# Selected attention's queries by token: x stationary, 16 of 64 columns rotated, turned by block

## The chip, the cores and the metric

The kernel runs on one core of a Trainium2 chip. Its metric is the device time in microseconds of one execution; the median of three runs stands for the kernel. The profile comes from one further execution. Its times start at the first instruction of the span.

## The reference, cut to what matters

One sequence of 512 tokens with 1024 features runs through two blocks. The first block's mixing part is where the change lies:

```python
h = rmsnorm(x, norm_mix_g)
proj = h @ w_in            # q 8x64, k 64, v 64, qi 4x64, ki 64, wi 4, glu 1024
q = partial_rope(q.reshape(bsz, seq, 8, 64), cos, sin)   # first 16 of 64 columns a head
# the same for k, qi, ki
# index scores: relu(qi . ki) weighted by wi; each query keeps its 128 best keys
logits = einsum('bqhd,bqkd->bqhk', q, k_sel) * 64 ** -0.5   # selected keys, causal
a_out = softmax(logits) @ v_sel
u = causal_dwconv(ga * sigmoid(gg), conv_b_w, conv_b_b)     # 31 taps, 512 channels
b_out = silu(layernorm(u))
x = x + concat([a_out, b_out]) @ w_out
```

`partial_rope` takes columns x1 = 0..7 and x2 = 8..15 of a head to x1 cos - x2 sin and x2 cos + x1 sin, and leaves the other 48 alone. After this come a cross-attention to 256 memory tokens (their keys and values, kc and vc, are made in fills during the selected attention), a feed-forward part, and the whole second block (a recurrent part, an attention without softmax, a feed-forward part). The diff touches none of these.

## The kernel before

Features lie on the partitions, tokens on the free axis, so an activation is a set of tiles of 128 x 512. Every projection is done in three passes on TensorE (PE) with a high and a low part of each operand: w_high x_high, w_high x_low, w_low x_high. Weights come in chunks of 128 x 1024 through two buffers (`weights_raw`, and by it `weights_high` and `weights_low`): SP issues the load, ACT makes the high part (`high`, L703), POOL subtracts (`low`, L625), PE multiplies (`chunk`, L1736). The cast of a chunk waits for the chunk two before it to be done.

Each engine walks the same list, `FIRST_PLAN` (L390 and on), and does what is its own in each item, strictly in that order. Items: ("tile", n, ...) is the n-th 128 columns of w_in (16 tiles: ki/wi, qi, k/v, glu and gate, and last q in 12 to 15); ("best",) is one round of the selection on DVE, three MAX8 and three replacements (L1291, L1294), 16 in all; ("chosen",) turns the scores into 0 or -1e30 (L1299); ("fill", n, ...) is half a chunk of the memory's keys or values (24 matmuls of 256 columns a chunk of kc); ("tap", i) is one tap of the convolution on DVE (L1235), 84 in all; ("product", i) is one on ACT (L788) that POOL adds (L674), 40 in all; steps 0 to 34 are the selected attention, 32 pairs of a block of 128 queries and a head: ("logits", j) on PE (L1953) and the mask on DVE (L1321) and exponential on ACT (L840), ("prob", j) the transposes by PE (L1961) and ACT's copy (L848), ("value", j) on PE (L1972).

The queries are made like every other tile: the weights stand in PE, x moves, ACT copies the tile of 128 columns x 512 tokens to `qT` (L763). The rotation of tile 12 + i is a matmul with a constant matrix `rotate` (("query_turn", 2 + i), L1920, 128x512 in full precision, two passes) into a bank of its own, and then on DVE three operations over 128x512 (`rope`, L1189 to L1191): bank x sine, qT x cosine, sum, though 48 of 64 columns are not changed by it. The sine and cosine tables lie by feature and hold 1/rms of each token. The index queries (tiles 1 and 2) are rotated in the same way, the keys similarly (`key_rope`).

Of the kernel before, what the change touches and what calls it, by code (L numbers as in the profile page):

```python
# [12 lines left out]
P = 128  # L13
T = 512
# [27 lines left out]
for _name, _n in GEMMS:  # L42
    CHUNK[_name], TILE[_name] = _c, _t
    _c += _n
    _t += _n // 2 if _name.startswith("down") or _name == "vc" else 2 * _n if _name in ("out", "oc", "out2") else _n
# [43 lines left out]
def build(nc, w8, w11, xT, memT, mem, positions, params, blockdiag, out):  # L89
    ctx = ExitStack()  # L90
    with ctx:
# [69 lines left out]
        wi = sb("wi", [P, QB, IDX_HEADS], where=s1)  # L161
        cosine = sb("cosine", [P, T], where=s1)
# [72 lines left out]
        angle = aux[4][:]  # L235
        x_square = ([aux[5][:]] + [gate[:, k] for k in range(1, 4)] + [score[:, k] for k in range(3)]
# [45 lines left out]
        rotated = sem("rotated")  # L282
        roped = sem("roped")
# [102 lines left out]
        def adds_before(i):  # L386
# [4 lines left out]
                      ("tile", 3, 2, 5), ("spread",), ("key_turn", 0), ("query_turn", 0), ("tile", 3, 5, KB),  # L391
                      ("wi",), ("query_turn", 1), ("mem_scale", 0, 4), ("key", 0), ("query", 0), ("query", 1),
                      ("tile", 4, 0, KB), ("mem_scale", 4, 8)]
        for n in range(len(INDEX)):
# [9 lines left out]
                   11: [("glu_scale", 7), ("glu", 2), ("best",), ("product", 2)],  # L404
                   12: [("gate", 3), ("best",), ("product", 3), ("product", 4)],
                   13: [("glu", 3), ("best",), ("best",), ("query", 2), ("product", 5)],
                   14: [("best",), ("query", 3), ("product", 6), ("product", 7)],
                   15: [("best",), ("best",), ("query", 4), ("product", 8), ("product", 9)]}
        FIRST_PLAN += BETWEEN[5]
        for n in range(6, 16):  # L410
            FIRST_PLAN.append(("tile", n, 0, 4))
            if n >= 13:
                FIRST_PLAN.append(("query_turn", n - 11))
            FIRST_PLAN += [("tile", n, 4, KB)] + BETWEEN[n]
# [37 lines left out]
        BANKS = [item for item in FIRST_PLAN if item[0] in ("prob", "heads")]  # L452
# [127 lines left out]
        def _(pool):  # L580
# [14 lines left out]
            for t in (rotate, twice, rotate_twice, causal, strict, ident16):  # L595
# [5 lines left out]
                                 fill=-1.0, base=-8, pattern=[[-HALF, 2], [-1, 8]], channel_multiplier=1))  # L601
# [9 lines left out]
                                 fill=-1.0, base=-8, pattern=[[0, 2], [-1, 8]], channel_multiplier=1))  # L611
# [81 lines left out]
        def _(act):  # L693
# [54 lines left out]
            def tile_ends(n):  # L748

                if n < 4:  # L750
                    dst = (None, None, qiT[:, 1], kv[:])[n]
                elif n < 12:
                    b = n // 2 - 2
                    dst = gate[:, b] if n % 2 else glu[:, b, TAPS - 1:TAPS - 1 + T]
                else:
                    dst = qT[:, n - 12]
                tile_done(n // 2, n % 2)
                if n < 4:
                    a.copy(dst, acc[:, n % 2]).then_inc(tile_out[n % 2], 1)
                    high_next(n // 2, n % 2)  # L760
                else:
                    high_next(n // 2, n % 2)
                    a.copy(dst, acc[:, n % 2]).then_inc(tile_out[n % 2], 1)  # L763
# [27 lines left out]
            for what, *n in FIRST_PLAN:  # L791
# [343 lines left out]
        def _(dve):  # L1135
# [102 lines left out]
            for what, *n in FIRST_PLAN:  # L1238
# [4 lines left out]
                elif what == "spread":  # L1243
                    dve.wait_ge(x_spread, 1)
                    dve.wait_ge(tables_ready, 1)
# [20 lines left out]
                elif what == "query":  # L1266
                    t = qiT[:, j] if j < 2 else qT[:, j - 2]
                    dve.wait_ge(table_copied, 1)
                    rope(t, t, aux[4][:], aux[2 + j if j < 2 else j - 2][:])
# [444 lines left out]
        def _(pe):  # L1714
# [112 lines left out]
            def in_tile(n, k, end):  # L1827
                m, s = n // 2, n % 2
                if k == 0:
                    free(s, m)  # L1830
                chunk(m, s, end, s, A, first=k)

# [31 lines left out]
            def bank_free(*item):  # L1864

                at = BANKS.index(item)
                if at >= 2:
                    kind, j = BANKS[at - 2]
                    if kind == "heads":
                        pe.wait_ge(inverse_out, j + 1)  # L1870
                    else:
                        pe.wait_ge(probT_ready, j + 1)
# [18 lines left out]
            for what, *n in FIRST_PLAN:  # L1891
# [12 lines left out]
                elif what == "spread":  # L1904
                    pe.wait_ge(x_factor, 1)
                    spread(tok_factor, aux[5]).then_inc(x_spread, 1)
                elif what == "key_turn":
                    if j:
                        pe.wait_ge(rel_used, len(INDEX))
                    pe.wait_ge(tile_out[j], (1, 2)[j])  # L1910
# [4 lines left out]
                elif what == "query_turn":  # L1915
                    tile = 1 + j if j < 2 else 10 + j
                    pe.wait_ge(tile_out[tile % 2], tile // 2 + 1)
                    if j >= 2:
                        pe.wait_ge(roped, 4)
                    t_.matmul(aux[2 + j if j < 2 else j - 2][:], rotate[:], qiT[:, j] if j < 2 else qT[:, j - 2],  # L1920
                              start=True, stop=True).then_inc(rotated, 1)
# [24 lines left out]
                elif what == "logits":  # L1946
                    qb, h = DSA[j]
                    if j < A_HEADS:
                        pe.wait_ge(roped, 5 + h // 2 if j >= 2 else 6)
# [5 lines left out]
                elif what == "prob":  # L1955
                    pe.wait_ge(prob_raw, j + 1)
                    if j < 2:
                        pe.wait_ge(roped, 8)
# [379 lines left out]
```

## Time and profile before

| what | us |
|---|---|
| median of three runs | 1372.78 (1372.58 to 1373.69) |
| the profiled execution, its own time | 1372.61 |
| its span, first to last instruction | 1370.6 |
| PE busy | 1331.1 |
| DVE busy | 790.1 |
| POOL busy | 612.0 |
| ACT busy | 549.5 |

A busy time is the time in which an engine had an instruction under way. Matmuls overlap, so two of 0.39 us may start 0.23 us apart: starts are what to count. PE is near full for the whole span; the others are not, but they hold PE up where the work of a stage hangs on them. So the table only says that PE's idle time and PE's own instructions matter.

### The profile page before, as it was taken

The numbers are of one execution on the slowest core, as the hardware profiler recorded it, in microseconds if no ns is written. First come the engines' busy times: TensorE is split into PE (matmuls) and PEld (weight loads), VectorE is DVE, ScalarE is ACT, GpSimd is POOL, SyncE is SP. The second block draws the span as 40 slices with busy tenths as digits, with TensorE's granted clock in tenths as the row PEclk, the third lists the DMA queues.
The fourth block names the chain that finished last, engine by engine and source line by source line (L and its number), as shares of the span: only waits on it lengthen the run. The fifth ranks groups of instructions, "written<-read, shape, count | busy, mean of one in ns | idle before, by whom it ended". The sixth has DMA issues, their size and how long they took to land. (4 is left out here: it accounts for less than half of the span.)

```text
span 1370.6 us, 18053 instructions
## 1 busy us (share of the span) xinstructions
PE 1331.1 (97%) x6189; PEld 1079.0 (79%) x6189; DVE 790.1 (58%) x1097; ACT 549.5 (40%) x860; POOL 612.0 (45%) x299
## 2 busy tenths in 40 slices
PE   8998889999999999999999999899999999999997
PEld 6787766887678888888888777688788888888886
DVE  7788896632456777777533588677543333332222
ACT  5444776542343222323323254455442233232322
POOL 4597873332234444444444534132344444444441
PEclk9999999999999999999999999999999999999999
DMA  6122321221122222323322222111122222233222
GB/s 227 62 93 93 108 75 34 92 78 62 46 92 88 98 92 96 103 92 109 106 87 97 92 77 77 46 47 62 62 93 92 97 102 92 92 109 105 95 87 80
DMA packets 31875, 121.19 MB, mean 88 GB/s; under 512 B 3536, under 2 KB 3664, under 8 KB 31568
## 3 DMA queue, kind: packets, MB, share of 16 engines
q1 hardware_dynamic: 31536, 119.81, 25.9%
q8 instruction: 32, 0.52, 0.2%
q10 hardware_dynamic: 288, 0.69, 0.2%
q14 instruction: 19, 0.16, 0.0%
HBM read 118.40 MB, written 2.10 MB: 88 GB/s over the span
## 5 line engine op out<-in xcount | busy, mean ns | idle before, releaser
L625 POOL TENSOR_TENSOR weights_low<-weights_raw,weights_high 128x1024 fp32r<-128x1024 f32 (+1 forms) x204 | 526.4, 2581 | 725.3 <-ACT weights_high L703 725.1
L703 ACT CAST weights_high<-weights_raw 128x1024 fp32r<-128x1024 f32 (+1 forms) x202 | 221.9, 1099 | 504.7 <-PE acc L1736 475.1
L1736 PE MATMUL acc<-a_high,weights_high 128*128 128x512 f32 x976 | 390.5, 400 | 1.8 <-DVE a_low L1398 1.1
L1736 PE MATMUL acc<-a_high,weights_low 128*128 128x512 f32 x976 | 380.6, 390 | 0.0
L1736 PE MATMUL acc<-a_low,weights_high 128*128 128x512 f32 x976 | 380.3, 390 | 0.0
L1736 PEld LDWEIGHTS acc<-a_high,weights_high 128*128 128x128 f32 x976 | 183.7, 188 | 44.1 <-issue 3.7
L1736 PEld LDWEIGHTS acc<-a_low,weights_high 128*128 128x128 f32 x976 | 183.7, 188 | 39.3 <-issue 2.6
L1736 PEld LDWEIGHTS acc<-a_high,weights_low 128*128 128x128 f32 x976 | 183.5, 188 | 38.7
L1208 DVE TENSOR_TENSOR residual<-acc,residual 128x512 f32<-128x512 f32 (+1 forms) x63 | 43.3, 687 | 168.4 <-PE acc L1736 129.8
L1736 PE MATMUL acc<-h_high,weights_high 128*128 128x512 f32 x330 | 128.9, 391 | 0.0
L1736 PE MATMUL acc<-h_high,weights_low 128*128 128x512 f32 x330 | 128.4, 389 | 0.0
L1736 PE MATMUL acc<-h_low,weights_high 128*128 128x512 f32 x330 | 128.4, 389 | 0.0
L1480 DVE TENSOR_TENSOR h_low<-work,h_high 128x512 f32 x44 | 88.9, 2020 | 39.5 <-ACT h_high L953 39.5
L1474 DVE TENSOR_TENSOR work<-acc,row_factor 128x512 f32<-128x512 f32 x44 | 30.4, 691 | 105.5 <-PE acc L1736 105.5
L1736 PEld LDWEIGHTS acc<-h_high,weights_low 128*128 128x128 f32 x330 | 61.9, 188 | 13.0
L1736 PEld LDWEIGHTS acc<-h_high,weights_high 128*128 128x128 f32 x330 | 62.0, 188 | 12.7
L1736 PEld LDWEIGHTS acc<-h_low,weights_high 128*128 128x128 f32 x330 | 62.0, 188 | 12.5
L950 ACT ACTIVATE work<-work 128x512 f32<-128x512 f32 x44 | 27.8, 631 | 96.7 <-DVE work L1471 93.5
L1394 DVE TENSOR_TENSOR square_sum<-square_sum,square 128x512 f32<-128x512 f32 x19 | 54.9, 2891 | 18.0 <-ACT square L1104 9.1
L1235 DVE SCALAR_TENSOR_TENSOR aux<-glu,par,aux 128x512 f32<-128x512 f32 x78 | 58.7, 753 | 1.7
L1469 DVE SCALAR_TENSOR_TENSOR work<-gated,par,work 128x512 f32<-128x512 f32 x22 | 55.4, 2518 | 3.4 <-DVE work L1467 3.4
L674 POOL TENSOR_TENSOR conv<-conv,product 128x512 f32<-128x512 f32 x38 | 49.4, 1300 | 10.4 <-ACT product L788 9.0
(384 smaller groups left out, 1932.8 us busy)
## 6 DMA issues: line engine op xcount, KB each, us to landing
weights_raw<-w SPq DMA_DIRECT2D x172, 512.0 KB, 3.2
weights_raw<-w SPq DMA_DIRECT2D x32, 704.0 KB, 4.1
residual<-xT SPq DMA_DIRECT2D x8, 256.0 KB, 6.1
out<-y_tok SPq DMA_DIRECT2D x4, 512.0 KB, 3.1
mem_raw<-memT SPq DMA_DIRECT2D x1, 1024.0 KB, 5.3
mem_tok<-mem SPq DMA_DIRECT2D x1, 1024.0 KB, 7.5
lru_weights<-blockdiag ACTq DMA_DIRECT2D x1, 512.0 KB, 3.3
sine<-positions SPq DMA_DIRECT2D x1, 256.0 KB, 6.7
```

Of the source, the lines that this page charges most:

```text
L625: g.tensor_tensor(weights_low[:, s, 0:cols], weights_raw[:, s, 0:cols], weights_high[:, s, 0:cols].bitcast(F32), ALU.subtract).then_inc(we ...
L674: g.tensor_tensor(conv[:, b], conv[:, b], product[:, j % 2], ALU.add).then_inc(last_conv_steps, 1)
L703: a.copy(weights_high[:, s, 0:cols], weights_raw[:, s, 0:cols]).then_inc(weight_high, 1)
L950: a.activation(work[:, 0], work[:, 0], ACT.Silu).then_inc(silu_ready, 1)
L1208: v.tensor_tensor(residual[:, bass.ds(n, 1)].rearrange("p a n -> p (a n)"), acc[:, s], residual[:, bass.ds(n, 1)].rearrange("p a n -> p (a ...
L1235: ins = v.scalar_tensor_tensor(dst, src, weight, sofar, ALU.mult, ALU.add)
L1394: v.tensor_tensor(total_ if to is None else to, total_, squares, ALU.add).then_inc(summed, 1)
L1469: own.then(v.scalar_tensor_tensor(work[:, 0], gated[:, 1:1 + T], dcol("fconv_w", c + 1), work[:, 0], ALU.mult, ALU.add))
L1474: v.tensor_tensor(work[:, 1], acc[:, 1], row_factor[:], ALU.mult).then_inc(tile_out[1], 1)
L1480: v.tensor_tensor(at(dst_low, i), work[:, 1], at(dst_high, i).bitcast(F32), ALU.subtract).then_inc(operand_low, 1)
L1736: last = t_.matmul(acc[:, bank, 0:cols], w[:, s, wide], x_[:, k0 + k, 0:cols], start=start and k == opens and n == 0, stop=stop and k == c ...
```

## The change

- Chunks 12 to 15 of w_in are stored in another layout: rows of 128 features with all 512 query columns, two such rows a chunk. In `query_chunk` a block of 128 tokens of x is the stationary operand and 512 columns of weights move. The four blocks of tokens add up in four banks (`aux[0]` to `aux[3]`) over all 96 matmuls.
- ACT copies each block out with the token's factor 1/rms (`query_out`), into the space of the index queries and keys, now unused. By token, a head's 16 rotated columns are a strided view; DVE rotates only these (`query_rope`, three operations of 128 elements a partition). PE turns the block with four transposes and ACT copies it to `qT` (`query_back`).
- The tables by token come at the start: eight transposes of 16 x 128 and a copy on ACT (`tables`), ahead of the spread of the token factors. The sign of the sine moves from the matrix into the frequencies.
- Block 0 is turned ahead of the first logits, blocks 1 to 3 in steps 1 to 6. The logits of block qb wait for its copy into `qT`.
- The four rotation matmuls and twelve 128x512 operations of the queries go. The selection rounds stand one or two places earlier in the list.
- Eight of the 84 taps come ahead of step 0; the other 76 are spread over the same 31 steps.

```diff
         FIRST_PLAN = [("tile", 0, 0, KB), ("tile", 1, 0, KB), ("tile", 2, 0, KB), ("tile", 3, 0, 2), ("sum",),
-                      ("tile", 3, 2, 5), ("spread",), ("key_turn", 0), ("query_turn", 0), ("tile", 3, 5, KB),
+                      ("tile", 3, 2, 5), ("tables",), ("spread",), ("key_turn", 0), ("query_turn", 0), ("tile", 3, 5, KB),
...
-                   11: [("glu_scale", 7), ("glu", 2), ("best",), ("product", 2)],
-                   12: [("gate", 3), ("best",), ("product", 3), ("product", 4)],
-                   13: [("glu", 3), ("best",), ("best",), ("query", 2), ("product", 5)],
-                   14: [("best",), ("query", 3), ("product", 6), ("product", 7)],
-                   15: [("best",), ("best",), ("query", 4), ("product", 8), ("product", 9)]}
+                   11: [("glu_scale", 7), ("glu", 2), ("best",), ("best",), ("product", 2)],
+                   12: [("gate", 3), ("best",), ("best",), ("product", 3), ("product", 4)],
+                   13: [("glu", 3), ("best",), ("best",), ("product", 5)],
+                   14: [("best",), ("best",), ("product", 6), ("product", 7)],
+                   15: [("product", 8), ("product", 9)]}
...
-        FIRST_PLAN += FILLS[:1] + [("query_turn", 5), ("best",), ("query", 5), ("chosen",)]
-        FILLS = FILLS[1:]
-        FILLS_AT = (2, 1, 2, 1, 2, 1, 2, 1, 1, 1, 2, 1, 1, 1, 1, 1, 1, 1, 0, 1, 1, 0, 1, 0,
+        TAPS_AHEAD = 8
+        FIRST_PLAN += [("chosen",)] + [("tap", i) for i in range(TAPS_AHEAD // 2)]
+        FIRST_PLAN += [("query_out", b) for b in range(QB)] + [("query_rope", 0)] + FILLS[:2]
+        FIRST_PLAN += [("query_back", 0)] + [("tap", i) for i in range(TAPS_AHEAD // 2, TAPS_AHEAD)]
+        FILLS = FILLS[2:]
+        FILLS_AT = (1, 1, 2, 1, 2, 1, 2, 1, 1, 1, 2, 1, 1, 1, 1, 1, 1, 1, 0, 1, 1, 0, 1, 0,
...
             if step < CONV_STEPS:
-                FIRST_PLAN += [("tap", i) for i in range(step * len(CONV) // CONV_STEPS,
-                                                         (step + 1) * len(CONV) // CONV_STEPS)]
+                rest = len(CONV) - TAPS_AHEAD
+                FIRST_PLAN += [("tap", TAPS_AHEAD + i) for i in range(step * rest // CONV_STEPS,
+                                                                      (step + 1) * rest // CONV_STEPS)]
+            if step in (1, 3, 5):
+                FIRST_PLAN.append(("query_rope", (step + 1) // 2))
+            if step in (2, 4, 6):
+                FIRST_PLAN.append(("query_back", step // 2))
...
+                elif what == "tables":
+                    act.wait_ge(tables_turned, 1)
+                    a.copy(token_tables[:].rearrange("p a b r -> p (a b r)"), aux[0][:, 0:2 * QB * 16]
+                           ).then_inc(token_tables_out, 1)
+                elif what == "query_out":
+                    if j < QB - 1:
+                        act.wait_ge(q_done, j + 1)
+                    else:
+                        act.wait_ge(chunk_done, 16)
+                    act.wait_ge(x_factor, 1)
+                    a.activation(q_tok[j], aux[j][:], ACT.Copy, scale=tok_factor[:, j:j + 1]).then_inc(q_out, 1)
+                elif what == "query_back":
+                    act.wait_ge(q_turned, j + 1)
+                    a.copy(qT[:, :, j * P:(j + 1) * P], turn_bank(what, j)[:].rearrange("p (n t) -> p n t", t=P)
+                           ).then_inc(q_ready, 1)
...
+                elif what == "query_rope":
+                    dve.wait_ge(token_tables_out, 1)
+                    dve.wait_ge(q_out, j + 1)
...
+                    own.step(v.tensor_tensor(turned_, heads_[:, :, ::-1, :], sines, ALU.mult))
+                    own.then(v.tensor_tensor(straight, heads_, cosines, ALU.mult))
+                    v.tensor_tensor(heads_, turned_, straight, ALU.add).then_inc(q_roped, 1)
...
+            def query_chunk(n, i):
+
+                if n == 12 and i == 0:
+                    pe.wait_ge(roped, 4)
+                pe.wait_ge(weight_low, n + 1)
+                for b in range(QB):
+                    rows, wide = slice(b * P, (b + 1) * P), slice(i * T, (i + 1) * T)
+                    for p_, (w, x_) in enumerate(((weights_high, a_high), (weights_high, a_low),
+                                                  (weights_low, a_high))):
+                        last = t_.matmul(aux[b][:], x_[:, 2 * (n - 12) + i, rows], w[:, n % 2, wide],
+                                         start=n == 12 and i == 0 and p_ == 0,
+                                         stop=n == 15 and i == 1 and p_ == 2)
+                    if n == 15 and i and b < QB - 1:
+                        last.then_inc(q_done, 1)
+                if i:
+                    last.then_inc(chunk_done, 1)
...
+                elif what == "tables":
+                    pe.wait_ge(tables_ready, 1)
+                    for i, table in enumerate((sine, cosine)):
+                        for b in range(QB):
+                            at = (i * QB + b) * 16
+                            last = t_.transpose(aux[0][:, at:at + 16], table[0:16, b * P:(b + 1) * P],
+                                                ident[0:16, 0:16])
+                    last.then_inc(tables_turned, 1)
+                elif what == "query_back":
+                    pe.wait_ge(q_roped, j + 1)
+                    if j == 0:
+                        pe.wait_ge(q_out, QB)
+                    bank_free(what, j)
+                    blocks_of(q_tok[j], turn_bank(what, j)).then_inc(q_turned, 1)
...
-                    if j < A_HEADS:
-                        pe.wait_ge(roped, 5 + h // 2 if j >= 2 else 6)
+                    if h == 0:
+                        pe.wait_ge(q_ready, qb + 1)
...
-    starts += every[:4]
+    queries = w_in[:, 0:T].reshape(4, 2, P, T).transpose(0, 2, 1, 3).reshape(4, P, -1)
```

## Rows read from the trace of the kernel before

**Rows 1.** The page: busy time, share of the span, instructions.
```profile
PE 1331.1 (97%) x6189; PEld 1079.0 (79%) x6189; DVE 790.1 (58%) x1097; ACT 549.5 (40%) x860; POOL 612.0 (45%) x299
```

**Rows 2.** Stretches (us from start:end): length, busy per engine, granted clock, DMA.
```profile
core 0: us, PE busy (x) PEld busy (x) DVE busy (x) ACT busy (x) POOL busy (x), PEclk, DMA share, GB/s
98.00:117.80 19.80, 19.80 (x84) 15.28 (x83) 14.40 (x36) 8.21 (x12) 17.08 (x12) 1.00 0.31 103
...
125.80:129.20 3.40, 0.00 (x0) 0.01 (x1) 3.29 (x8) 3.40 (x6) 2.48 (x2) 1.00 0.00 0
...
130.00:133.40 3.40, 3.40 (x19) 3.40 (x18) 0.01 (x1) 0.76 (x3) 3.40 (x3) 0.52 0.48 154
...
160.00:221.00 61.00, 54.53 (x308) 42.04 (x307) 56.36 (x104) 44.55 (x96) 42.59 (x28) 1.00 0.18 62
...
228.00:1370.60 1142.60, 1120.31 (x5105) 909.61 (x5103) 603.94 (x700) 415.17 (x605) 454.10 (x177) 1.00 0.26 86
```

**Rows 3.** Timeline of PE around a rotation: start, length, engine, line, operation, count.
```profile
101.24 0.39 PE L1736 MATMUL acc<-a_high,weights_low 128*128 128x512 f32 x1
101.47 1.02 PE L1920 MATMUL aux<-qT,rotate 128*128 128x512 f32 x2
...
102.55 0.39 PE L1736 MATMUL acc<-a_low,weights_high 128*128 128x512 f32 x1
```

**Rows 4.** Timeline of PE, last query tile to the third fill; idle before in brackets.
```profile
117.54 0.39 PE L1736 MATMUL acc<-a_high,weights_low 128*128 128x512 f32 x1
...
120.59 0.38 PE L1953 MATMUL aux<-kT,qT 128*128 128x128 f32 x2
...
129.22 0.36 PE L1736 MATMUL acc<-m_high,weights_high 128*128 128x256 f32 x1 [3.44 <-POOL weights_low L625]
...
133.67 0.28 PE L1736 MATMUL acc<-m_high,weights_low 128*128 128x256 f32 x1
```

**Rows 5.** Timeline of PE, four transposes and what follows them.
```profile
223.42 0.60 PE L1961 MATMUL aux<-ident,prob 128*128 128x128 f32 x4
223.86 1.06 PE L1972 MATMUL aux<-probT,v_pad 128*128 128x128 f32 x8
```

**Rows 6.** Timeline of DVE, first rotation of a query tile to the first mask.
```profile
102.60 0.70 DVE L1189 TENSOR_TENSOR aux<-aux,sine 128x512 f32<-128x512 f32 x1 [4.02 <-PE aux L1920]
...
110.98 1.48 DVE L1291 MAX8 small<-score 128x8 f32<-128x256 f32 x3
...
113.95 1.47 DVE L1291 MAX8 small<-score 128x8 f32<-128x256 f32 x3
...
123.95 0.90 DVE L1299 TENSOR_SCALAR score<-score 128x256 f32<-128x256 f32 x3
124.88 0.29 DVE L1321 CUSTOM_DVE_ANT_0 masked<-aux,causal 128x128 f32<-128x128 f32 x1
```

**Rows 7.** Timeline of ACT from the end of the last query tile.
```profile
118.04 1.05 ACT L703 CAST weights_high<-weights_raw 128x1024 fp32r<-128x1024 f32 x1 [3.57 <-PE acc L1736]
...
120.92 1.28 ACT L831 ACT_TABLE_LOAD   x1
...
125.61 1.03 ACT L703 CAST weights_high<-weights_raw 128x1024 fp32r<-128x1024 f32 x1
```

**Rows 8.** POOL: timeline at chunk 20; its waits from 135 to 157.6 us (total, times, longest).
```profile
135.17 2.39 POOL L625 TENSOR_TENSOR weights_low<-weights_raw,weights_high 128x1024 fp32r<-128x1024 f32 x1 [1.27 <-ACT weights_high L703]
...
POOL weights_low L625 <- ACT weights_high L703: 1.3, 1, 1.3
```

**Rows 9.** Groups: the taps from 134 to 228 us, and ACT's copies of vc.
```profile
L1235 DVE SCALAR_TENSOR_TENSOR aux<-glu,par,aux 128x512 f32<-128x512 f32 x74 | 55.7, 753 | 1.6
...
L774 ACT ACTIVATE vc<-acc,small x4: 672/678/681, 179.4 to 228.4; 128x512 f32<-128x512 f32 x4
```

**Rows 10.** Who waited for whom: PE from 157 to 221, ACT from 134 to 228.
```profile
PE aux L1972 <- ACT probT L848: 4.6, 6, 1.3
PE aux L1961 <- ACT probT L848: 1.7, 1, 1.7
...
ACT prob L840 <- DVE small L1321: 21.2, 21, 2.0
```

More of the change, by code:

```diff
@@ L44 @@
     _c += _n
-    _t += _n // 2 if _name.startswith("down") or _name == "vc" else 2 * _n if _name in ("out", "oc", "out2") else _n
+    _t += (_n // 2 if _name.startswith("down") or _name == "vc" else 2 * _n if _name in ("out", "oc", "out2")
+           else 12 if _name == "in" else _n)
 CHUNKS, TILES = _c, _t
@@ L161, in build @@
         wi = sb("wi", [P, QB, IDX_HEADS], where=s1)
+        token_tables = sb("token_tables", [P, 2, QB, 16], where=s1)
         cosine = sb("cosine", [P, T], where=s1)
@@ L282, in build @@
         rotated = sem("rotated")
+        tables_turned = sem("tables_turned")
+        token_tables_out = sem("token_tables_out")
+        q_done = sem("q_done")
+        q_out = sem("q_out")
+        q_roped = sem("q_roped")
+        q_turned = sem("q_turned")
+        q_ready = sem("q_ready")
         roped = sem("roped")
@@ L451, in build @@
         FIRST_PLAN += [("ln_low", 2), ("ln_low", 3)] + FIRST[10:]
-        BANKS = [item for item in FIRST_PLAN if item[0] in ("prob", "heads")]
+        BANKS = [item for item in FIRST_PLAN if item[0] in ("prob", "heads", "query_back")]
         def turn_bank(*item):
@@ L760, in tile_ends @@
                     high_next(n // 2, n % 2)
+                elif n < 12:
+                    high_next(n // 2, n % 2)
+                    a.copy(dst, acc[:, n % 2]).then_inc(tile_out[n % 2], 1)
                 else:
                     high_next(n // 2, n % 2)
-                    a.copy(dst, acc[:, n % 2]).then_inc(tile_out[n % 2], 1)
             def fill_ends(n):
@@ L1266, in _ @@
                 elif what == "query":
-                    t = qiT[:, j] if j < 2 else qT[:, j - 2]
                     dve.wait_ge(table_copied, 1)
-                    rope(t, t, aux[4][:], aux[2 + j if j < 2 else j - 2][:])
+                    rope(qiT[:, j], qiT[:, j], aux[4][:], aux[2 + j][:])
+                elif what == "query_rope":
+                    dve.wait_ge(token_tables_out, 1)
+                    dve.wait_ge(q_out, j + 1)
+                    span = slice(j * P, (j + 1) * P)
+                    heads_ = q_tok[j].rearrange("p (h g e) -> p h g e", g=8, e=8)[:, :, 0:2, :]
+                    sines, cosines = (token_tables[:, i, j].rearrange("p (a g e) -> p a g e", a=1, g=2)
+                                      .broadcast_to([P, A_HEADS, 2, 8]) for i in range(2))
+                    turned_, straight = (t[:, span].rearrange("p (h g e) -> p h g e", g=2, e=8)
+                                         for t in (sine, cosine))
+                    own.step(v.tensor_tensor(turned_, heads_[:, :, ::-1, :], sines, ALU.mult))
+                    own.then(v.tensor_tensor(straight, heads_, cosines, ALU.mult))
+                    v.tensor_tensor(heads_, turned_, straight, ALU.add).then_inc(q_roped, 1)
                 elif what == "index":
@@ L1827, in in_tile @@
             def in_tile(n, k, end):
+                if n >= 12:
+                    query_chunk(n, k // 4)
+                    return
                 m, s = n // 2, n % 2
@@ L1915, in _ @@
                 elif what == "query_turn":
-                    tile = 1 + j if j < 2 else 10 + j
+                    tile = 1 + j
                     pe.wait_ge(tile_out[tile % 2], tile // 2 + 1)
[L1918 to L1921, printed above, removed]
+                    t_.matmul(aux[2 + j][:], rotate[:], qiT[:, j], start=True, stop=True).then_inc(rotated, 1)
                 elif what == "wi":
@@ L1956, in _ @@
                     pe.wait_ge(prob_raw, j + 1)
-                    if j < 2:
-                        pe.wait_ge(roped, 8)
                     bank_free(what, j)
@@ L2297 @@
     w8 = np.concatenate([
-        _column_blocks(w_in, starts), _column_blocks(a["w_k_cross"][0], d),
+        _column_blocks(w_in, starts), queries, _column_blocks(a["w_k_cross"][0], d),
         _row_pairs(a["w_v_cross"][0]), out1,
```

20 lines of the change are left out of this document (10 added, 10 removed).

## The prediction

> **What bounds the kernel now.** I read the busy shares first, then the stretches around the changed code, then what each engine stood idle for there. TensorE (PE) is busy 1331.1 us of a span of 1370.6 [rows 1], so what matters is its own work and the few places where it stands. The 1142.6 us behind 228 us are untouched by the diff and have PE busy 1120.3 us [rows 2]. All that can change lies before 228. There I see four parts with different limits:
>
> - Tiles 12 to 15, 98 to 117.8 us: PE busy 19.80 of 19.80 us [rows 2]. PE's own count of instructions decides.
> - The start of the selected attention: PE does nothing from 125.8 to 129.2 us, then its granted clock is 0.52 from 130 to 133.4, that is 1.2 GHz instead of 2.4 [rows 2]. PE waited there for POOL's weights_low [rows 4], POOL for ACT's cast at 125.61, and that cast stood behind the first exponential, which waited for DVE's first mask at 124.88 [rows 6, 7]. DVE was late because it still had selection rounds, two rotations and the 0/-1e30 step to do. So DVE is the cause, through three queues.
> - 135 to 157.5 us: POOL waits only once, 1.3 us, and works the rest without a gap [rows 8]. It sets the pace.
> - 160 to 221 us: DVE is busy 56.36 of 61 us, PE 54.53 [rows 2]. PE stands for ACT's copies of the turned probabilities, 4.6 and 1.7 us in seven waits, and ACT in turn stands 21.2 us for DVE's masks [rows 10]. DVE sets the pace, PE has 6.5 us idle to give.
>
> **The change part by part.**
>
> *Start, tables by token.* Eight transposes of 16 x 128 on PE at about 32 us, where PE is without a gap. The nearest row is a group of four 128x128 transposes: it starts at 223.42 and what follows at 223.86, 0.44 us for four [rows 5]. Eight cost 0.9 us if the 128-column weight load is what they cost (I take this), 0.4 us if a transpose of 16 columns costs half. ACT's copy of 128 columns ends while PE still spreads the token factors, so the new wait of the key rotation costs nothing; without that cover it would be 0.3 us. **+0.9 us.**
>
> *Query matmuls.* 4 chunks x 2 halves x 4 blocks x 3 passes = 96 matmuls of 512 columns, as before (4 x 8 x 3 = 96). Which operand is stationary does not change the count, each still loads 128 columns and moves 512. No change. The bytes loaded and SP's queue are the same.
>
> *Four rotation matmuls go.* The row before the first starts at 101.24; the second pass of the next block starts at 102.55, where two steps of 0.225 would put it at 101.69: 0.86 us each [rows 3]. Three of them stand inside tiles 13 to 15: **-2.6 us**. The fourth stands in the stretch after it and is counted there. The last matmul of tile 15, at 117.54 before [rows 4], starts at 117.5 + 0.9 - 2.6 = 115.8.
>
> *DVE ahead of the queries.* DVE had done 12 of its 16 selection rounds when it stood 4.02 us for the first rotation until 102.60 [rows 6]. A round is 113.95 - 110.98 = 2.97 us. The rotations no longer stand in DVE's queue, so the rounds run through: 98.6 + 0.9 + 4 x 2.97 = 111.4, the 0/-1e30 step 0.9 more, four taps of 0.75 [rows 9] to 115.4. DVE is then free 9 us earlier than before, and stands until the first query block is out.
>
> *The new serial chain.* Behind tile 15 ACT has the cast of the next chunk (0.95), two products (0.63 and 0.8) and the table load with the small exponential (1.5), as before from 118.04 to 122.4 less the copy of 0.5 [rows 7]; from 116.3 that is 120.2. Then four copies out of PSUM with a factor by token. The nearest row is the copy of vc, 0.678 us, same shape and form [rows 9]; back to back it is 0.59, so all four are out at 122.55. DVE's rotation of a block is three operations of 128 elements a partition; a mask of 128 columns takes 0.29 [rows 6], so 0.75 us with its waits (between 0.6, and 2.1 by the 0.70 of the 512-column rotation), and block 0 has it by 121.6, hidden behind the later copies. PE has meanwhile only fill 0, 24 matmuls of 0.119 = 2.9 us, done at 119.0. It stands from 119.0 to 122.6, turns block 0 (0.45), and stands again until ACT has made the next cast (0.95), which is ahead of it, and the copy into qT (0.5): the first logits start at 124.15. Before they started at 120.59 [rows 4]. Two stands of 3.6 and 1.1 us against one of 3.4.
>
> *Clock.* Before, PE stood 3.4 us and some 0.8 us after it went on the clock was 0.52 for 3.4 us [rows 2]. I take the same here: low from about 123.4 to 126.8, of which 2.6 us is work, so 1.3 us lost. *What PE has done by then:* from 124.15 come the logits of steps 0 to 2 (0.22 each), the halves of fills 1 and 2 (four of 1.43) and a transpose, 6.5 us; with the clock's 1.3 fill 2 ends at 132.0, where before its last matmul starts at 133.67 [rows 4]. Chunk 18 is low by 126 (cast 122.6 to 123.5, POOL 2.4), ahead of its use; chunk 19 by 131.2. **Fill 2 ends 1.8 us earlier** (this holds the -2.6, the +0.9, the fourth rotation and the new stands). Without the clock's fall it would be 3.2. With a rotation of 2.1 us nothing moves, since it runs while ACT copies. DVE's first mask is at 125.0, as before at 124.88 [rows 6], but now with eight taps behind it.
>
> *The POOL stretch.* POOL's subtraction of chunk 20, at 135.17 before [rows 8], starts 1.8 us earlier; POOL's work per step is unchanged and continuous, so the lead is held and not added to. The other three turns of query blocks (0.45 us of PE and 0.5 of ACT each) and rotations (0.75 of DVE each) lie in steps 1 to 6 beside it, at nothing; if POOL did not set the pace there, 1.4 us of PE.
>
> *Eight taps ahead.* In steps 11 to 30 DVE had 55 taps, now 34 to 83, 50 taps. Five of 0.753 [rows 9] are 3.8 us less for DVE, from 160 to 221, where it sets the pace. PE can give at most 6.5. At the 0.92 busy share of DVE there I take **-3.5 us**; at least 0 (the handshakes decide), at most 6.5.
>
> A row shows that transposes come 0.11 us apart, each lasting 0.27 and overlapping the next [rows 5]. The Trainium skill (TensorE: Matmul & The Clock Gate, PE-mode transpose) gives some 275 ns for one in a kernel and says that transposes do not count as busy to the clock. By that figure, taken as the interval, the 24 new transposes would cost an estimated 6.6 us and not 2.6. The trace agrees with it as a duration and not as an interval.
>
> Sum: -1.8 - 3.5 = -5.3 us. The profiled execution took 1372.61 (2.0 beside its span), 0.17 under the median 1372.78. 1372.6 - 5.3 = **1367.3**.
>
> **Rivals.**
>
> 1. *Handshakes, not DVE's load, set steps 11 to 30.* For it: PE's waits name ACT's copy, and DVE still has gaps there. Against: ACT stands 21.2 us for DVE [rows 10]. Then only the 1.8 and a little remain: 1370.5.
> 2. *No clock fall and a full gain.* The stand is broken by four transposes; DVE's lead takes away nearly all of PE's idle time: -3.2 - 5.2, 1364.2.
> 3. *Transposes in their new place cost their length* (0.27 each, not 0.11). For it: they stand alone between waits. Against: rows 5. Of the 24, the eight of the tables and the four of block 0 are on PE's path, +1.9, the others +1.3 where POOL doesn't hide them: -5.3 + 3.2 = -2.1, 1370.5. The skill's section above is this rule.
> 4. *Slower: the serial chain behind tile 15 costs more than the stall it replaces.* ACT has six things before the first logits, and PE stands for each. If the clock stays low through both stands and beyond (a second fall of 3.4 us, 1.7 lost), and the cast of chunk 19, behind the exponential of step 1, puts POOL's work 2 to 3 us later than I have it, fill 2 ends 2.7 us later than before instead of 1.8 earlier; with nothing from the taps, 1372.6 + 2.7 = 1375.3. It decides from where POOL starts chunk 20 behind 138 (135.17 before). For it: two stands of 4.7 us together against 3.4.
>
> **How the numbers follow.** A change of 0.2% is 2.7 us, about what can be told from none. Forecast 0.55 (its own range 1365.2 to 1369.4, the clock's 1.4 and 0.7 of the taps either way), rival 1 0.17, rival 2 0.15, rival 3 0.03, rival 4 0.10. Faster (under 1370.0): 0.55 + 0.15 = 0.70. Same: 0.20. Slower 0.10. The range is 1363.8 to 1372.0; it leaves out rival 4 and the upper end of rival 1.
>
> **What would show it.** Right: no rotation matmuls among the tiles, 8 short transposes near 32 us; the last query matmul near 115.8; four copies from PSUM at 120 to 122.6 on ACT; PE idle near 119 to 122.6; low clock once, before 127; POOL's chunk 20 near 133.4; the last mask some 5.3 us earlier. The taps' step is wrong if the stretch from step 11 to the last mask takes as long as before. The chain's step is wrong if the first logits start elsewhere than 124. The prediction as a whole is wrong if PE's idle time between 119 and 134 exceeds 6 us, or if anything behind the first output projection takes another time.

## The result, and the profile after

The changed kernel takes 1375.62 us (1375.06 to 1377.35), the kernel before 1373.43 in the same sessions: 1.0018 times as long, 95% interval 1.0011 to 1.0025. That is 2.2 us slower where 5.3 us faster was forecast, and outside the range.

The profiled execution was the slowest of its 14 (1377.35). Most of its extra 1.7 us over the median lie at 776 us, where PE's matmuls ran at half the clock for 3.4 us. The profiled execution of the kernel before has no such stretch there, but three of the ten experiments below have it at the same place in the code. All readings of the trace below are therefore taken before 230 us. The first matmul of the convolution's mean serves as a marker behind the changed code: it starts at 227.47 before and at 229.72 after, 2.25 us later, as much as the whole difference of the medians.

Stretches of the changed kernel, columns as in [rows 2]:

```profile
118.70:122.40 3.70, 0.12 (x2) 0.02 (x1) 1.73 (x5) 3.69 (x7) 2.09 (x2) 0.82 0.36 142
...
123.30:127.60 4.30, 3.62 (x17) 3.43 (x17) 3.23 (x6) 1.69 (x4) 3.29 (x2) 0.50 0.17 40
...
134.80:138.00 3.20, 3.17 (x15) 3.18 (x16) 3.13 (x9) 2.90 (x7) 1.32 (x1) 0.50 0.34 132
...
160.00:220.00 60.00, 55.87 (x314) 43.62 (x314) 53.76 (x102) 46.56 (x99) 45.05 (x30) 1.00 0.21 71
```

There are now two stretches at 1.2 GHz, where [rows 2] had one. The first goes from 121.1 us (hence the 0.82 of the first line) to 127.9, the second from 134.6 to 138.2. Both begin while PE stands, that is, has nothing to run, as its timeline shows:

```profile
32.06 0.42 PE L1975 MATMUL aux<-ident,sine 16*128 16x16 f32 x4
32.33 0.39 PE L1975 MATMUL aux<-ident,cosine 16*128 16x16 f32 x4
...
115.56 0.39 PE L1886 MATMUL aux<-weights_low,a_high 128*128 128x512 f32 x1
...
122.41 1.08 PE L1896 MATMUL aux<-ident,qiT 128*128 128x128 f32 x4 [3.59 <-ACT kiT L829]
124.17 0.80 PE L2029 MATMUL aux<-kT,qT 128*128 128x128 f32 x2 [0.68 <-ACT qT L832]
...
134.83 1.12 PE L1896 MATMUL aux<-ident,qiT 128*128 128x128 f32 x4 [2.21 <-DVE qiT L1310]
...
151.21 0.66 PE L1896 MATMUL aux<-ident,kiT 128*128 128x128 f32 x4 [1.54 <-DVE kiT L1310]
```

The last query matmul starts 2.0 us earlier than in [rows 4] (forecast 1.7), and the first logits at 124.17 (forecast 124.15). Up to there only the clock, low already from 121.1, is unexpected. Then PE stands 2.2 and 1.5 us for DVE's rotations of blocks 1 and 3. DVE's timeline has block 0's rotation and parts of the later ones:

```profile
120.64 0.30 DVE L1308 TENSOR_TENSOR sine<-qiT,token_tables 128x128 f32<-128x128 f32 x1 [5.49 <-ACT qiT L829]
120.86 0.28 DVE L1309 TENSOR_TENSOR cosine<-qiT,token_tables 128x128 f32<-128x128 f32 x1
121.17 0.29 DVE L1310 TENSOR_TENSOR qiT<-sine,cosine 128x128 f32<-128x128 f32 x1
...
131.24 1.94 DVE L1308 TENSOR_TENSOR sine<-qiT,token_tables 128x128 f32<-128x128 f32 x1
133.10 1.34 DVE L1309 TENSOR_TENSOR cosine<-qiT,token_tables 128x128 f32<-128x128 f32 x1
134.48 0.29 DVE L1310 TENSOR_TENSOR qiT<-sine,cosine 128x128 f32<-128x128 f32 x1
...
147.42 2.47 DVE L1309 TENSOR_TENSOR cosine<-kiT,token_tables 128x128 f32<-128x128 f32 x1
```

And POOL's at the same times:

```profile
130.64 2.39 POOL L640 TENSOR_TENSOR weights_low<-weights_raw,weights_high 128x1024 fp32r<-128x1024 f32 x1 [2.72 <-ACT weights_high L718]
132.99 1.31 POOL L689 TENSOR_TENSOR conv<-conv,product 128x512 f32<-128x512 f32 x1
...
147.30 2.44 POOL L640 TENSOR_TENSOR weights_low<-weights_raw,weights_high 128x1024 fp32r<-128x1024 f32 x1
```

The same instruction takes 0.28 us or 2.47. Where it is long, it ends just after the instruction that POOL has under way: 131.24 + 1.94 = 133.18 behind POOL's 133.03, 133.10 + 1.34 = 134.44 behind 134.30, 147.42 + 2.47 = 149.89 behind 149.74. In block 0, POOL's addition ended at 120.79, 0.15 us into the first operation, which ended at 120.94; the other two had POOL idle. The nine operations of blocks 1 to 3 take 11.0 us together and not 9 x 0.29 = 2.6; seven of the nine are long, from 0.83 to 2.47 us.

### The profile page after: what moved, and what is told of

Same layout as the page of the kernel before. It is cut to its first block and busy times, and to the rows that moved or that the text cites. A ratio compares the mean times of both kernels' runs of the same rounds, so it can differ in the third digit from the quotient of the medians.

```text
span 1374.3 us, 18085 instructions
## 1 busy us (share of the span) xinstructions
PE 1332.3 (97%) x6205; PEld 1082.1 (79%) x6205; DVE 793.0 (58%) x1097; ACT 552.4 (40%) x865; POOL 613.0 (45%) x299
## 5 line engine op out<-in xcount | busy, mean ns | idle before, releaser
L1777 PE MATMUL acc<-a_high,weights_high 128*128 128x512 f32 x944 | 377.2, 400 | 1.8 <-DVE a_low L1439 1.1
L1777 PE MATMUL acc<-a_high,weights_low 128*128 128x512 f32 x944 | 369.0, 391 | 0.0
L1777 PE MATMUL acc<-a_low,weights_high 128*128 128x512 f32 x944 | 368.6, 390 | 0.0
L1777 PEld LDWEIGHTS acc<-a_high,weights_high 128*128 128x128 f32 x944 | 177.9, 188 | 42.4 <-issue 3.0
L1777 PEld LDWEIGHTS acc<-a_high,weights_low 128*128 128x128 f32 x944 | 177.8, 188 | 37.5
L1777 PEld LDWEIGHTS acc<-a_low,weights_high 128*128 128x128 f32 x944 | 178.0, 189 | 37.2 <-issue 1.9
```

The costliest lines, as they stand in the source:

```text
L1777: last = t_.matmul(acc[:, bank, 0:cols], w[:, s, wide], x_[:, k0 + k, 0:cols], start=start and k == opens and n == 0, stop=stop and k == c ...
```

## Experiments

Theory A: an operation of DVE that has both inputs in SBUF stands still until POOL's instruction is over; the rotations put into the steps run into it. Theory B: the stand ahead of the first logits, with its clock, is what costs. Times are medians; each was timed beside the kernel before, which had 1373.6 to 1373.75 us in these sessions (1373.43 in the change's own).

The table has for each version the median, the start of the marker in its one profiled execution, and how long the granted clock was 1.2 GHz in that execution, in two parts of the kernel:

| version | us (runs; lowest to highest) | marker | 1.2 GHz, 110 to 145 us | 1.2 GHz, 760 to 896 us |
|---|---|---|---|---|
| kernel before | 1373.43 (14; 1372.58 to 1374.17) | 227.47 | 3.4 | 3.4 |
| changed kernel | 1375.62 (14; 1375.06 to 1377.35) | 229.72 | 10.2 | 6.8 |
| 1, rotations ahead | 1371.94 (11; 1370.30 to 1374.58) | 225.28 | 3.4 | 6.8 |
| 2, one operand from PSUM | 1370.46 (7; 1368.42 to 1372.56) | 224.52 | 6.8 | 6.8 |
| 3, rotations left out | 1370.22 (11; 1369.12 to 1371.15) | 223.79 | 6.8 | 6.8 |
| 4, no taps ahead | 1379.66 (5; 1378.46 to 1379.92) | 233.24 | 10.3 | 6.8 |
| 5, PE kept busy | 1373.29 (11; 1372.62 to 1375.45) | 227.56 | 0 | 3.4 |
| 6, taps ahead of the copies | 1370.52 (11; 1369.30 to 1372.85) | 223.75 | 6.8 | 6.8 |
| 7, fill 1 split | 1367.35 (5; 1365.97 to 1369.51) | 221.02 | 0 | 3.4 |
| 8, as 9, rotation from SBUF | 1371.18 (11; 1370.06 to 1373.30) | 225.67 | 6.8 | 3.4 |
| 9, rotation from the banks | 1364.35 (5; 1364.30 to 1365.85) | 219.17 | 0 | 3.4 |
| 10, as 9, copies late | 1369.54 (8; 1367.47 to 1373.44) | 223.07 | 3.4 | 6.8 |

The last column is in code that is the same in all of them. From the marker to the end of the span it is 1142.9 to 1143.4 us where that column has 3.4, and 1144.3 to 1144.7 where it has 6.8. So 1.4 us of an execution's time can have nothing to do with an edit, and a difference of two medians is not good to much less than 1 us; the marker is free of this part.

**1. Rotations ahead.**

```diff
-        FIRST_PLAN += [("query_out", b) for b in range(QB)] + [("query_rope", 0)] + FILLS[:2]
+        FIRST_PLAN += [("query_out", b) for b in range(QB)] + [("query_rope", b) for b in range(QB)] + FILLS[:2]
...
-            if step in (1, 3, 5):
-                FIRST_PLAN.append(("query_rope", (step + 1) // 2))
```

> All four token rotations stand behind the copies out of PSUM, at about 121 to 123.3 us where POOL is idle, instead of one there and three in steps 1, 3 and 5; nothing else moves. Theory A (an operation of DVE with two SBUF operands stands still while POOL's instruction runs; the three rotations in the steps took 3.5, 2.8 and 4.5 us instead of 0.8): each now takes 0.8, PE's waits of 2.2 and 1.5 us for them go, and the second fall of the clock at 134.8 with them; 4 to 6 us under the changed kernel, 1369.5 to 1371.5, faster than the kernel before. Theory B (the stand of 3.6 us ahead of the first logits and its clock are what costs): the stand stays, DVE's first mask comes 2 us later, so 1376 or more.

1371.94 us, 0.9989 of the kernel before (0.998 to 0.9998), 3.7 under the changed one (4.4 by the marker), 0.4 above the top of what theory A gave. The waits for the rotations are gone and so is the second fall. Eleven of the twelve operations took 0.28 to 0.30. The twelfth began 0.08 us behind POOL, and the first mask came only at 128.95 (125.13 in the changed kernel); first DVE, then POOL:

```profile
123.24 2.42 DVE L1308 TENSOR_TENSOR kiT<-sine,cosine 128x128 f32<-128x128 f32 x1
```
```profile
123.16 2.36 POOL L638 TENSOR_TENSOR weights_low<-weights_raw,weights_high 128x1024 fp32r<-128x1024 f32 x1 [2.49 <-ACT weights_high L716]
```

**2. One operand from PSUM, same place.**

```diff
...
-                    own.step(v.tensor_tensor(turned_, heads_[:, :, ::-1, :], sines, ALU.mult))
-                    own.then(v.tensor_tensor(straight, heads_, cosines, ALU.mult))
-                    v.tensor_tensor(heads_, turned_, straight, ALU.add).then_inc(q_roped, 1)
+                    banked = aux[5][:, 0:P].rearrange("p (h g e) -> p h g e", g=2, e=8)
+                    dve.wait_ge(conv_steps, taps_done[0])
+                    own.step(v.tensor_tensor(turned_, heads_[:, :, ::-1, :], banked, ALU.mult))
+                    own.then(v.tensor_tensor(straight, heads_, banked, ALU.mult))
+                    v.tensor_tensor(heads_, turned_, banked, ALU.add).then_inc(q_roped, 1)
+                    dve.wait_ge(q_roped, j + 1)
...
```

> The rotations stay where the change has them, three operations over the same strided columns, but the second operand of each is read from the convolution's bank in PSUM instead of the tables and the second product, so the queries' rotation is not computed. Theory A (one SBUF operand leaves POOL alone): each operation takes 0.3 us wherever it stands, the time falls by 3 to 5 us from the changed kernel's 1375.6. A rival (the strided and reversed view is slow by itself, or DVE waits for a semaphore): they take as long as in the changed kernel, 1375 to 1377.

1370.46 us, 5.2 under the changed kernel, by the marker as well, 0.2 more than theory A gave at most. All twelve operations took 0.28 or 0.29, over the same reversed and strided view. DVE's timeline for block 1, in the place where it took 3.5:

```profile
131.90 0.29 DVE L1311 TENSOR_TENSOR sine<-qiT,aux 128x128 f32<-128x128 f32 x1
132.11 0.28 DVE L1312 TENSOR_TENSOR cosine<-qiT,aux 128x128 f32<-128x128 f32 x1
132.43 0.29 DVE L1313 TENSOR_TENSOR qiT<-sine,aux 128x128 f32<-128x128 f32 x1
```

And POOL's:

```profile
131.08 2.40 POOL L640 TENSOR_TENSOR weights_low<-weights_raw,weights_high 128x1024 fp32r<-128x1024 f32 x1 [3.68 <-ACT weights_high L718]
```

POOL's subtraction was under way for all three. So the long durations are neither the view nor a semaphore. This is the experiment that decides for theory A.

**3. Rotations of blocks 1 to 3 left out.**

```diff
+                    if j:
+                        v.memset(turned_[:, 0:1, 0:1, :], 0.0).then_inc(q_roped, 1)
+                        continue
```

> The rotations of blocks 1 to 3 are left out (a memset of 8 elements signals in their place); block 0 as it is. Theory A: this is the price of the three in the steps, 4 to 6 us with the clock's second fall, so 1369.5 to 1371.5, and within 1 us of the version with all rotations ahead. Theory B: no more than DVE's 2 us, 1374 to 1375.

1370.22 us, 5.4 under the changed kernel and 0.2 under the one with a PSUM operand. The three rotations cost 5.4 us as they stand (5.9 by the marker), and little when POOL does not hold them: 0.2 by the medians, 0.7 by the marker. The stand ahead of the logits is no part of that, since it is the same 3.6 us here and the clock is low behind it for the same 6.8 us.

**4. No taps ahead.**

```diff
-        TAPS_AHEAD = 8
+        TAPS_AHEAD = 0
```

> The changed kernel with all 84 taps spread over the steps again, none ahead. By the prediction's step the eight taps ahead are worth 3.5 us in steps 11 to 30: 1379 us. If handshakes and not DVE's load set these steps, 1375.6 to 1376.5. Against it, four taps fewer ahead of the first mask would let it come no earlier, since the first logits end the wait there.

1379.66 us, 4.0 over the changed kernel. DVE's masks of step 8 and step 31 (the first and the last over the scores), first the changed kernel, then this one:

```profile
155.51 0.42 DVE L1362 CUSTOM_DVE_ANT_0 masked<-aux,score 128x256 f32<-128x256 f32 x1
...
221.81 0.69 DVE L1362 CUSTOM_DVE_ANT_0 masked<-aux,score 128x512 f32<-128x512 f32 x1
```
```profile
155.97 0.42 DVE L1362 CUSTOM_DVE_ANT_0 masked<-aux,score 128x256 f32<-128x256 f32 x1
...
225.97 0.68 DVE L1362 CUSTOM_DVE_ANT_0 masked<-aux,score 128x512 f32<-128x512 f32 x1
```

66.30 us with eight taps ahead, 70.00 without; the kernel before has 150.23 and 220.21, 69.98. From the mask of step 11, where the prediction counted, to the last it is 56.92, 60.63 and, before, 60.61. DVE's load set these steps, rival 1 is out.

**5. PE kept busy in its stand.**

```diff
+                    if j == 0:
+                        free(1, TILE["kc"] // 2)
+                        for i in range(14):
+                            t_.matmul(acc[:, 1], a_high[:, i % 8, 0:P], a_high[:, i % 8], start=True, stop=True)
```

> The changed kernel with 14 more matmuls of 128x512 (3.2 us, into a bank whose content nobody reads) where PE stands 3.6 us for the copies of the queries; they change no wait. If the stand is what lowers the clock, it stays at 1.2 GHz nowhere between 121 and 129 and the first two fills behind it run in half the time: 1.5 to 2.5 us under 1375.6, so 1373.1 to 1374.1. If the clock falls for another reason or the time is DVE's anyway, no change within 0.7 us.

1373.29 us, 2.3 under the changed kernel (2.2 by the marker) and level with the one before (1.0001, 0.9992 to 1.001). Stretches and timeline of PE:

```profile
122.40:130.00 7.60, 6.90 (x57) 6.66 (x58) 6.82 (x14) 4.52 (x9) 5.19 (x3) 1.00 0.21 71
130.00:140.00 10.00, 6.91 (x55) 6.33 (x55) 9.82 (x19) 3.97 (x10) 7.12 (x5) 1.00 0.31 105
```
```profile
118.61 3.36 PE L1982 MATMUL acc<-a_high 128*128 128x512 f32 x14
122.36 0.63 PE L1896 MATMUL aux<-ident,qiT 128*128 128x128 f32 x4 [0.39 <-ACT kiT L829]
...
132.67 0.66 PE L1896 MATMUL aux<-ident,qiT 128*128 128x128 f32 x4 [2.20 <-DVE qiT L1310]
```

The first fall is gone, and so is the second, although the stand of 2.2 us is still there: the stand that was followed by a fall in the changed kernel was followed by none in this one profile. So the stand ahead of the logits does cost, by way of the clock. The 2.3 us are the price of both falls together; the wait itself is still there, filled with work that nobody needs. Theory B is true for these 2.3 us, but not enough for the result by itself.

**Towards a faster version.** Three more, each on top of the one before it. The sixth starts from the first experiment and puts all eight taps ahead of the copies (DVE stood 5.5 us there), the seventh also splits fill 1 around the turn of block 0. The edit of the seventh against the changed kernel, without the lines of the first experiment's edit in the steps:

```diff
-        FIRST_PLAN += [("chosen",)] + [("tap", i) for i in range(TAPS_AHEAD // 2)]
-        FIRST_PLAN += [("query_out", b) for b in range(QB)] + [("query_rope", 0)] + FILLS[:2]
-        FIRST_PLAN += [("query_back", 0)] + [("tap", i) for i in range(TAPS_AHEAD // 2, TAPS_AHEAD)]
-        FILLS = FILLS[2:]
-        FILLS_AT = (1, 1, 2, 1, ...
+        FIRST_PLAN += [("chosen",)] + [("tap", i) for i in range(TAPS_AHEAD)]
+        FIRST_PLAN += [("query_out", b) for b in range(QB)] + [("query_rope", b) for b in range(QB)] + FILLS[:3]
+        FIRST_PLAN += [("query_back", 0)] + FILLS[3:4]
+        FILLS = FILLS[4:]
+        FILLS_AT = (0, 0, 2, 1, ...
...
```

> All rotations ahead as in the first experiment, and all eight taps in the 5.5 us in which DVE stands for the first copy, instead of four there and four behind the rotations. In the first experiment the first mask came at 128.95, since DVE had the last rotation (caught by POOL, 2.4 us) and four taps (3.1 us) before it. Now it comes at 126: 2 to 3 us less than 1371.9, so 1369 to 1370, if DVE sets the start; no change if PE's fills and POOL's chunk 19 do.

1370.52 us, 1.4 under the first: less than the 2 to 3 us expected. The first mask came 3.2 us earlier (125.79 for 128.95), so more than half of that was given back behind it, before POOL's chunk 20 (134.48 for 136.01, only 1.5 us earlier). The clock was low for 6.8 us in this profile and for 3.4 in that of the first; that this is the cause is not shown.

> The sixth with the first two halves of fill 1 moved out of steps 0 and 1: one ahead of the turn of block 0 (in PE's stand of 3.6 us), one behind it (in the stand of 0.7 us for the copy). Chunk 17 is low at 119.5, so PE still stands some 1 us, then works. If PE's order sets the start: 1.5 to 2.5 us under the sixth, 1367 to 1368, the clock's fall included. If DVE and POOL do (84 taps and 16 chunks have not changed), no more than 0.5 us.

1367.35 us, 3.2 less than the sixth (2.7 by the marker). PE stands 1.03 us for the copies and 1.81 for the first mask, and its clock is 1.00 throughout.

The ninth reads the banks in the rotation (the tables get 1/rms from one DVE operation at the start) and has ACT copy the queries out ahead of its products and the table load:

```diff
...
+                    own.then(v.tensor_tensor(turned_, bank_[:, :, ::-1, :], sines, ALU.mult))
+                    own.then(v.tensor_tensor(bank_, bank_, cosines, ALU.mult))
+                    v.tensor_tensor(heads_, turned_, bank_, ALU.add).then_inc(q_roped, 1)
...
-        FIRST_PLAN += [("query_back", 0)] + [("tap", i) for i in range(TAPS_AHEAD // 2, TAPS_AHEAD)]
+        FIRST_PLAN += [("product", 8), ("softplus",), ("query_back", 0), ("product", 9)] + FILLS[3:4]
...
```

> The seventh, and the rotation reads the four accumulator banks with tables that carry 1/rms, so that no operation of DVE has two SBUF operands; ACT copies the blocks out right behind its cast, ahead of the two products and the small exponential with its table load. Theory A: the twelve operations take 0.3 us each though POOL runs beside them. The copies end 3 us earlier, at 119.6, the first logits start at about 121 instead of 124. 1 to 3 us under the seventh: 1365 to 1367; the same as the seventh if POOL's chunks 18 and 19 set the start.

**1364.35 us, 0.9936 of the kernel before (0.9922 to 0.9949)**, 9.3 us faster than it and 11.3 than the change (8.3 and 10.6 by the marker), and 0.65 under the range expected. Unlike the second and third it does the whole computation. Its turn of block 0 starts at 121.58 with 0.41 us of stand, and its clock is 1.00 from 110 to 145. All twelve operations of the rotation took 0.28 to 0.30 us, and nine of them began while POOL had a subtraction under way; two of these, and POOL's:

```profile
120.91 0.30 DVE L1310 TENSOR_TENSOR aux<-aux,token_tables 128x128 f32<-128x128 f32 x1
121.24 0.29 DVE L1311 TENSOR_TENSOR kiT<-sine,aux 128x128 f32<-128x128 f32 x1
```
```profile
120.23 2.38 POOL L638 TENSOR_TENSOR weights_low<-weights_raw,weights_high 128x1024 fp32r<-128x1024 f32 x1 [0.87 <-ACT weights_high L716]
```

Two versions take its two parts away one at a time. The eighth goes back to the rotation from SBUF:

> The ninth kernel's order (copies of the queries right behind the cast, all rotations ahead, eight taps before them, fill 1 split around the turn), but the rotation as in the change, with two SBUF operands. It now runs from 118 on, where POOL has the low part of chunk 17 (117.0 to 119.4) and behind it an addition and chunk 18. Theory A: two or more of its twelve operations are caught, 2 to 5 us more of DVE ahead of the turn: 1 to 3 us over the version from the banks (1364.35), 1365.5 to 1367.5. If the rival held (PSUM operands are no different here), the same time as that version.

1371.18 us, 6.8 over the ninth (6.5 by the marker), far above what was expected. Four of twelve operations were caught, two of them:

```profile
121.15 2.37 DVE L1308 TENSOR_TENSOR qiT<-sine,cosine 128x128 f32<-128x128 f32 x1
...
125.25 2.43 DVE L1306 TENSOR_TENSOR sine<-kiT,token_tables 128x128 f32<-128x128 f32 x1
```

The first mask moved to 128.79 (124.05 in the ninth), PE stood 4.9 us for it, and the clock was 0.50 from 128.1 to 135.0. The four operations lost 6.5 us on DVE. About as much reached the end, but not by DVE's path alone: the low clock has a part in it that was not measured apart.

The tenth keeps the rotation from the banks and goes back to the late copies:

> The version from the banks with the copies of the queries behind the two products and the small exponential again, as in the change: 1364.35 plus what the order of ACT is worth. If PE's and POOL's start behind the copies sets the time, 2 to 3 us over it, 1366.5 to 1367.5, near the seventh (1367.35), since there the rotations are nearly free of POOL too.

1369.54 us (1367.47 to 1373.44, a wide spread), 5.2 over the ninth (3.9 by the marker) and 2.2 over the seventh. As in the ninth, the turn of block 0 waits for all four rotations (they write the banks that it needs). Behind the late copies PE stands 2.8 us for them, and the clock is 0.50 from 123.8 to 127.3. Copying out first is worth more than expected; it takes away this stand and this fall, and how much each is worth was not measured apart.

## Why the prediction was wrong

Point by point, by its steps:

- *Tables by token:* +0.9 forecast. The eight transposes take 0.6 us of PE (32.06 to the next at 32.66). Right in kind, 0.3 too high. So rival 3 is out: transposes cost their spacing, 0.08 us here and 0.11 in the turns of the query blocks, and not their length.
- *Query matmuls, rotation matmuls, DVE ahead, the serial chain:* 115.8, 115.4, 122.55 and 124.15 forecast; 115.56, 115.1, 122.3 and 124.17 measured. Right.
- *The clock:* one fall from 123.4 to 126.8 forecast, 3.4 us; it came inside the stand, at 121.1, and lasted until 127.9, and in the version without the rotations from 122.5 to 129.4, 6.8 us both times. POOL's chunk 20 starts at 134.48 there, 0.7 us before [rows 8], where 1.8 was forecast. So the term of -1.8 was 1.1 us too good even without the rotations. The longer fall is what it missed: chunk 19 was low at 133.0 (133.3 without the rotations) where 131.2 was forecast, and at 130.9 in the fifth experiment, which has no fall.
- *Rotations in the steps:* **the step that failed.** "The other three turns of query blocks (...) and rotations (0.75 of DVE each) lie in steps 1 to 6 beside it, at nothing". They took 3.5, 2.8 and 4.5 us, made PE stand 3.75 us in two waits, and a second fall of the clock followed. POOL's chunk 20 started at 136.68, 1.5 us later than before. Price by the third experiment: 5.4 us of time. Without them the time is 1370.2, inside the range, though 2.9 above the forecast. The upper bound (2.1) was also wrong: it came from an operation with a bank of PSUM as its input [rows 6], which POOL does not hold up. The 0.29 came from a mask, which reads a bank as well. A row of the kernel before had the answer, in its groups of DVE:

```profile
L1341 DVE TENSOR_TENSOR a_low<-att,a_high 128x512 fp32r<-128x512 f32 x3 | 4.3, 1434 | 2.5 <-ACT a_high L863 2.5
```

  The same size and kind as the 0.70 of [rows 6], both inputs in SBUF, twice as long. The page of the kernel before has it larger still, 44 operations with both inputs in SBUF and 44 with one in a bank:

```profile
L1480 DVE TENSOR_TENSOR h_low<-work,h_high 128x512 f32 x44 | 88.9, 2020 | 39.5 <-ACT h_high L953 39.5
L1474 DVE TENSOR_TENSOR work<-acc,row_factor 128x512 f32<-128x512 f32 x44 | 30.4, 691 | 105.5 <-PE acc L1736 105.5
```

  And the rotation of the kernel before was out of POOL's way. Besides its product in a bank it read a copy of the cosine table in a bank (`aux[4]`), so each of its three operations had one operand there. They took 0.68 to 0.70 us with POOL at work:

```profile
103.20 0.68 DVE L1190 TENSOR_TENSOR qT<-qT,aux 128x512 f32<-128x512 f32 x1
103.91 0.69 DVE L1191 TENSOR_TENSOR qT<-qT,aux 128x512 f32<-128x512 f32 x1
```
```profile
103.00 2.73 POOL L674 TENSOR_TENSOR conv<-conv,product 128x512 f32<-128x512 f32 x2
```

  The change moved queries, tables and products to SBUF and gave this up. A stretch in which POOL "works without a gap" is where such operations cost most, and I had used that fact only in favour of the change. The Trainium skill (SBUF — State Buffer, Who interferes with whom) has the rule: a DVE instruction with two SBUF inputs contends with a GpSimd (POOL) instruction that reads SBUF, since its second input comes through a read interface that the two share, and whichever comes first holds it for its whole instruction. The trace agrees where POOL came first, with 2.47 us against 0.28. Whether POOL waits in turn when DVE came first was not looked at.
- *Eight taps ahead:* -3.5 forecast, -3.7 measured from the mask of step 11 to that of step 31, 4.0 in time by the fourth experiment (3.5 by the marker). Right.

The last mask adds it up: 220.21 before, 215.90 without the three rotations (-4.3, forecast -5.3), 221.81 with them. Rival 4 forecast 1375.3, slower by the serial chain, and that its number is so near is luck. Its mark, POOL's chunk 20 behind 138, was not met (136.68), it had nothing from the taps, and the chain gave the first logits at 124.17, as forecast. It was right about the clock, which stayed low through both stands and beyond and fell once more. Both falls together cost 2.3 us by the fifth experiment, where the prediction had 1.3 for one. What decided was that DVE's rotations waited for POOL. The prediction's own alarm did not go off: PE was idle for 5.5 us between 119 and 134, under the 6 that it named, since the first wait for a rotation reaches beyond 134 (132.6 to 134.8) and the second ends at 151.2. Open is how much of the 5.4 us is DVE's delay and how much the second fall. PE was busy 3.17 of the 3.2 us from 134.8 to 138.0, so by an estimate from that row the fall cost at most some 1.7 us of its 3.5, and the larger part is the delay. In the fifth experiment, without the first fall, the second did not come.

## What to carry to other kernels

Before small DVE operations are put beside a busy POOL, look where their inputs lie: with two in SBUF each can cost the rest of a POOL instruction, whatever its own size (0.28 us became up to 2.47 here). Several small ones in a row can each be caught, as seven of nine were. Read one input from PSUM (it is often there already, in the accumulator), or place them where POOL is idle. When data moves to another layout, look at which operands leave PSUM by it: the kernel before had one there in each operation. And where PE must stand for a serial chain, give it work that does not depend on the chain: in the seventh version that saved 3.2 us, the halved clock included.

## What the runs showed of the hardware

- DVE tensor-tensor of 128 elements a partition: 0.28 to 0.30 us alone or with a PSUM input, 0.8 to 2.5 us with two SBUF inputs and POOL's 2.4 us subtraction or 1.3 us addition under way at its start. It then ended 0.14 to 0.15 us behind POOL's instruction.
- With a stand of PE of 3.6 us came 1.2 GHz for 6.8 us in five profiles and for 3.4 in one (the first experiment), with one of 4.9 us for 6.8 (the eighth), with one of 2.8 us for 3.4 (the tenth) and with one of 3.4 us for 3.4 (the kernel before). With a stand of 2.2 us came 1.2 GHz for 3.5 us in the changed kernel, and none where the first stand was filled with matmuls. Stands of 0.9, 1.0 and 1.8 us a few us apart left the clock at 2.4 GHz (the seventh).
- In four of the twelve profiled executions the clock fell for 3.4 us at one place in the second block (776 us in the changed kernel; the second, sixth and tenth experiments), with no stand of PE over 0.8 us in the 10 us ahead of it. In the other eight it did not fall there.
